# Two products of the first two layers moved from full fp32 to three passes over high and low parts

## What is computed

```python
h = modulate(rms_norm(x, norm1_g[l]), sh1, sc1)
...                                   # projections, gated linear attention -> o_a, differential attention -> o_b2
y_a = o_a @ w_a                       # (512 x 512) @ (512 x 1024)
y_b = o_b2 @ w_b                      # the second branch's product
merged = jax.nn.sigmoid(gate_a) * y_a + jax.nn.sigmoid(gate_b) * y_b
y = merged @ w_o                      # the output product, (512 x 1024) @ (1024 x 1024)
x = x + g1 * y
h = modulate(rms_norm(x, norm2_g[l]), sh2, sc2)
x = x + g2 * hier_moe(h, ...)         # router, then 2 of 32 experts for each token
```

## Time and profile before

| | us |
|---|---|
| median of 3 runs | 3723.69 (3720.17 to 3726.69) |
| the profiled execution's own time | 3723.39 |
| its span in the trace | 3721.7 |
| PE busy | 3159.5 (85%) |
| DVE, ACT, POOL busy | 1131.9, 962.3, 805.8 |
| bytes moved | 663.67 MB |

### The profile page before, as it was taken

How to read it: one execution, slowest core, us unless ns; L and a number is a source line. 1 busy time by engine, 2 the same in 40 slices (tenths; PEclk the granted TensorE clock), 3 DMA queues, 4 the chain that set the end, 5 groups by cost and what they waited for, 6 DMA issues and landing times. The chain is left out here.

```text
span 3721.7 us, 42396 instructions
## 1 busy us (share of the span) xinstructions
PE 3159.5 (85%) x15027; PEld 2046.8 (55%) x15027; DVE 1131.9 (30%) x2001; ACT 962.3 (26%) x1351; POOL 805.8 (22%) x382
## 2 busy tenths in 40 slices
PE   6988987888884798879688777588899998889999
PEld 4764644333332576454433333365688786568877
DVE  4464423111111446431311111134343303434330
ACT  4323311111111522330111111134333323433331
POOL 3311100111111221120011111230243343024432
PEclk7998997899997899889799999789899998989999
DMA  5223332899998122332499999610122331012232
GB/s 209 68 76 126 136 115 91 340 405 409 409 408 311 69 75 99 119 114 92 180 396 408 409 409 407 256 51 31 60 91 80 90 123 51 31 61 91 80 90 69
DMA packets 289710, 663.67 MB, mean 178 GB/s; under 512 B 20190, under 2 KB 114708, under 8 KB 289552
## 3 DMA queue, kind: packets, MB, share of 16 engines
q1 hardware_dynamic: 271680, 623.43, 45.1%
q0 software_dynamic: 17872, 38.14, 2.8%
HBM read 653.64 MB, written 25.69 MB: 183 GB/s over the span
## 5 line engine op out<-in xcount | busy, mean ns | idle before, releaser
L869 PE MATMUL psum<-s_parts 128*128 128x512 f32 (+1 forms) x3744 | 955.2, 407 | 119.5 <-POOL s_parts L757 39.2
L869 PEld LDWEIGHTS psum<-s_parts 128*128 128x128 f32 (+1 forms) x3744 | 723.3, 195 | 327.6 <-issue 85.6
L869 PE MATMUL psum<-s_ring,s_units 128*64 128x512 f32 x3168 | 743.8, 619 | 129.8 <-DMA s_ring<-in_w_expert_in 90.9
L847 POOL TENSOR_TENSOR s_parts<-s_ring,s_parts 128x4096 fp32r<-128x4096 f32 (+2 forms) x52 | 407.8, 7841 | 873.1 <-ACT s_parts L2068 873.1
L869 PEld LDWEIGHTS psum<-s_ring,s_units 128*64 128x64 f32 x3168 | 251.4, 141 | 578.8 <-issue 446.1
L869 PE MATMUL psum<-s_h_low,s_parts 128*128 128x512 f32 (+1 forms) x1872 | 470.7, 392 | 11.2 <-DVE s_hid_low L2039 11.2
L869 PEld LDWEIGHTS psum<-s_h_low,s_parts 128*128 128x128 f32 (+1 forms) x1872 | 350.6, 188 | 96.0 <-DVE s_hid_low L2039 12.1
L869 PE MATMUL psum<-s_units 128*128 (+9 forms) x1520 | 296.5, 412 | 99.1 <-DVE s_gsl L1829 34.3
L757 POOL TENSOR_TENSOR s_parts<-s_ring,s_parts 128x4096 fp32r<-128x4096 f32 (+1 forms) x22 | 180.4, 8200 | 685.0 <-ACT s_parts L2068 685.0
L2068 ACT ACTIVATE s_parts<-s_ring 128x4096 fp32r<-128x4096 f32 (+3 forms) x74 | 237.3, 3209 | 168.4 <-PE psum L869 103.7
L869 PEld LDWEIGHTS psum<-s_units 64*128 64x128 f32 (+3 forms) x1520 | 175.3, 193 | 178.7 <-issue 121.1
(11 more groups left out here) (350 smaller groups left out, 2664.4 us busy)
## 6 DMA issues: line engine op xcount, KB each, us to landing
s_ring<-in_w_expert_in SPq DMA_DIRECT2D x132, 2048.0 KB, 23.5
s_ring<-in_w_expert_out SPq DMA_DIRECT2D x66, 2048.0 KB, 24.6
s_ring<-in_w_in SPq DMA_DIRECT2D x28, 2048.0 KB, 8.8
s_ring<-in_w_ada SPq DMA_DIRECT2D x24, 2048.0 KB, 9.2
s_ring<-in_ffn_w_up SPq DMA_DIRECT2D x40, 1024.0 KB, 6.4
s_ring<-in_ffn_w_down SPq DMA_DIRECT2D x16, 1408.0 KB, 7.0
s_ring<-in_w_out SPq DMA_DIRECT2D x8, 2048.0 KB, 7.8
s_units<-ys_scratch POOLq DMA_DIRECT2D x16, 512.0 KB, 6.4
```

The source lines that it names most:

```text
L847: pool.tensor_tensor(parts[:, s, 0:size], ring[:, s, 0:size], parts[:, 4 + n % 2, 0:size].bitcast(F32), ALU.subtract).then_inc(weights_low ...
L869: return pe.matmul(o, lhsT=lhsT, rhs=rhs, start=start, stop=stop)
```

## The change

`yb` and `wo` become three passes over high and low parts. The activations of `yb` are split by four copies on ACT (into units 8 to 11) and four subtractions on DVE (over `dq` itself); those of `wo` by eight copies on ACT (into `h_hi`) and eight subtractions on DVE (into `h_low`, the memory of `hT`). The three weight blocks `yb`, `wo` 0 and `wo` 1 get their high parts from ACT and low parts from POOL like the others. The squares of the second norm go to units 0 to 7 instead of `hT`. The weights of the first two experts are loaded in another order: the middle blocks of both after `wo` 3, the second expert's other two and one of the first after `wo` 7, and the last one after `rt`.

```diff
-SPLIT_A = [..., ("gb", 0), ("gb", 1)]
+SPLIT_A = [..., ("gb", 0), ("gb", 1), ("yb",), ("wo", 0), ("wo", 1)]
...
+    dq_hi = [hid_low[:, 8 + k, :] for k in range(HEADS)]
+    dq_low = [units_high[:, 2 + k, :] for k in range(HEADS)]
...  SP
-                    sp.wait_ge(TA.done.sem, TA.done_at(l, RA.reader_last(s) if s < 3 else ("gb", 7)))
+                    sp.wait_ge(TA.done.sem, TA.done_at(l, RA.reader_last(s) if s < 3 else last_of_high[s]))
+        last_of_high = {3: ("wo", 7), 4: ("wo", 3), 5: ("wo", 7)}
...
-            for u in (1, 0):
-                expert(l, before * 2, u, u, True)
+            for u, pieces in ((0, (1,)), (1, (1,)), (1, (0, 2)), (0, (2, 0))):
+                expert(l, before * 2, u, u, True, pieces)
...  POOL
-            low_part(10)
+            for n in range(10, len(SPLIT_A)):
+                low_part(n)
...  PE
+            w = [x.rearrange("p k n -> p (k n)").rearrange("p (k n) -> p k n", k=4) for x in block_parts(("yb",))]
+            pe.wait_ge(dq_high.sem, dq_high.at(l, HEADS))
+            pe.wait_ge(dq_lowered.sem, dq_lowered.at(l, HEADS))
             for m in range(8):
-                fm(("yb", m), slot_view(RA.slot(("yb",)), 4, D), P * m, dq, 4)
+                o = opened(("yb", m))
+                for n, (a, rows) in enumerate(((0, dq_hi), (1, dq_hi), (0, dq_low))):
+                    for k in range(HEADS):
+                        last = mm(o, w[a][:, k, tok(m)], rows[k], n == 0 and k == 0, n == 2 and k == HEADS - 1)
+                done(last)
             for m in range(KD):
                 if m % 4 == 0:
+                    w = block_parts(("wo", m // 4))
-                if m == 0:
-                    pe.wait_ge(TA.by(("yb", 7)).sem, TA.freed_at(l, ("yb", 7)))
                 o = opened(("wo", m))
-                for k in range(KD):
-                    last = mm(o, wview(RA, ("wo", m // 4), KD, 512)[:, k, tok(m % 4)], mrg[k], k == 0, k == KD - 1)
+                for n, (a, b) in enumerate(TERMS):
+                    for k in range(KD):
+                        if m == 0 and n == 0:
+                            pe.wait_ge(merged_high.sem, merged_high.at(l, k + 1))
+                        if m == 0 and n == 2:
+                            pe.wait_ge(merged_low.sem, merged_low.at(l, k + 1))
+                        last = mm(o, w[a][:, k, tok(m % 4)], h_parts[b][:, k, :], n == 0 and k == 0, n == 2 and k == KD - 1)
                 done(last)
-            sumsq(("n2",), x_squared, KD)
+            sumsq(("n2",), x_squared, KD, U)
...  DVE
+            for h in range(HEADS):
+                ve.wait_ge(dq_high.sem, dq_high.at(l, h + 1))
+                ve.tensor_tensor(dq_low[h], dq[:, h, :], dq_hi[h].bitcast(F32), ALU.subtract).then_inc(dq_lowered.sem, dq_lowered.more())
+            def low_merged(m):
+                ve.wait_ge(merged_high.sem, merged_high.at(l, m + 1))
+                ve.tensor_tensor(h_low[:, m, :], mrg[m], h_hi[:, m, :].bitcast(F32), ALU.subtract).then_inc(merged_low.sem, merged_low.more())
             for m in range(8):
                 o = done(("yb", m))
...
                 ve.tensor_tensor(mrg[m], mrg[m], T[:, m % 2, :], ALU.add).then_inc(TA.by(("yb", m)).sem, TA.by(("yb", m)).more())
+                if m:
+                    low_merged(m - 1)
+            low_merged(7)
...  ACT
             high_part(10)
+            for h in range(HEADS):
+                ae.wait_ge(head_normed.sem, head_normed.at(l, 13 + h))
+                copy(dq_hi[h], dq[:, h, :]).then_inc(dq_high.sem, dq_high.more())
             for m in range(8):
+                if m == 4:
+                    high_part(11)
                 ae.activation(gate_b[m], done(("gb", m)), ACT.Sigmoid).then_inc(TA.by(("gb", m)).sem, TA.by(("gb", m)).more())
+            high_part(12)
+            for m in range(8):
+                ae.wait_ge(TA.by(("yb", m)).sem, TA.freed_at(l, ("yb", m)))
+                copy(h_hi[:, m, :], mrg[m]).then_inc(merged_high.sem, merged_high.more())
+            high_part(13)
-            squares(KD, lambda k: ae.wait_ge(TA.by(("wo", k)).sem, TA.freed_at(l, ("wo", k))))
+            squares(KD, lambda k: ae.wait_ge(TA.by(("wo", k)).sem, TA.freed_at(l, ("wo", k))), U)
```

More of the change, by code:

```diff
@@ L273, in blocks_b @@
     return [(name, last, s, None) for name, last, s in b]
-SPLIT_A = [("lr",), ("gqk",), ("gv",), ("gg",), ("dq",), ("dk",), ("dv",), ("ga", 0), ("ga", 1), ("gb", 0), ("gb", 1)]
+SPLIT_A = [("lr",), ("gqk",), ("gv",), ("gg",), ("dq",), ("dk",), ("dv",), ("ga", 0), ("ga", 1), ("gb", 0), ("gb", 1), ("yb",), ("wo", 0),
+           ("wo", 1)]
 SPLIT_B = [name for name, *_ in blocks_b()]
@@ L498, in program @@
     weights_made = sig("a_attention_weights", HEADS * NT)
+    dq_high, dq_lowered = sig("a_attention_high", HEADS), sig("a_attention_low", HEADS)
+    merged_high, merged_low = sig("a_merged_high", KD), sig("a_merged_low", KD)
     gates_made = sig("a_branch_a_gates", 3)
@@ L589, in _, with expert @@
         freed_in_m = (m_in_read[0], m_in_read[1], m_down_made)
-        def expert(l, number, e, u, layer_first):
-            for j in range(3):
+        last_of_high = {3: ("wo", 7), 4: ("wo", 3), 5: ("wo", 7)}
+        def expert(l, number, e, u, layer_first, pieces=range(3)):
+            for j in pieces:
                 s = 3 * u + j
                 if layer_first:
-                    sp.wait_ge(TA.done.sem, TA.done_at(l, RA.reader_last(s) if s < 3 else ("gb", 7)))
+                    sp.wait_ge(TA.done.sem, TA.done_at(l, RA.reader_last(s) if s < 3 else last_of_high[s]))
                     settle(sp)
@@ L944, in tm_parts, with sumsq @@
                 done(of_parts(o, lambda a, k: h_parts[a][:, k, tok(t)], lambda b, k: w[b][:, k, :]))
-            def sumsq(name, signal, first):
+            def sumsq(name, signal, first, rows=hT):
                 o = opened(name)
@@ L950, in sumsq @@
                     pe.wait_ge(signal.sem, signal.at(l, first + k + 1))
-                    last = mm(o, ones[:], hT[:, k, :], k == 0, k == KD - 1)
+                    last = mm(o, ones[:], rows[:, k, :], k == 0, k == KD - 1)
                 done(last)
@@ L1134, in _ @@
                 fm_parts(("gb", m), w, P * (m % 4))
-            pe.wait_ge(weights_in_a[RA.slot(("yb",))], RA.landed(l, ("yb",), ("rt",)))
-            pe.wait_ge(head_normed.sem, head_normed.at(l, 16))
+            w = [x.rearrange("p k n -> p (k n)").rearrange("p (k n) -> p k n", k=4) for x in block_parts(("yb",))]
+            pe.wait_ge(dq_high.sem, dq_high.at(l, HEADS))
+            pe.wait_ge(dq_lowered.sem, dq_lowered.at(l, HEADS))
             for m in range(8):
-                fm(("yb", m), slot_view(RA.slot(("yb",)), 4, D), P * m, dq, 4)
+                o = opened(("yb", m))
[3 more added lines that the diff above has]
+                done(last)
             for m in range(KD):
                 if m % 4 == 0:
-                    pe.wait_ge(weights_in_a[RA.slot(("wo", m // 4))], RA.landed(l, ("wo", m // 4), ("rt",)))
-                if m == 0:
-                    pe.wait_ge(TA.by(("yb", 7)).sem, TA.freed_at(l, ("yb", 7)))
+                    w = block_parts(("wo", m // 4))
                 o = opened(("wo", m))
-                for k in range(KD):
-                    last = mm(o, wview(RA, ("wo", m // 4), KD, 512)[:, k, tok(m % 4)], mrg[k], k == 0, k == KD - 1)
+                for n, (a, b) in enumerate(TERMS):
[5 more added lines that the diff above has]
+                        last = mm(o, w[a][:, k, tok(m % 4)], h_parts[b][:, k, :], n == 0 and k == 0, n == 2 and k == KD - 1)
                 done(last)
-            sumsq(("n2",), x_squared, KD)
+            sumsq(("n2",), x_squared, KD, U)
             o = opened(("rt",))
@@ L2084, in done, with squares @@
                 return psum[:, TA.bank(name), :]
-            def squares(first, ready):
+            def squares(first, ready, rows=hT):
                 for k in range(KD):
                     ready(k)
-                    ae.activation(hT[:, k, :], xT[:, k, :], ACT.Square).then_inc(x_squared.sem, x_squared.more())
+                    ae.activation(rows[:, k, :], xT[:, k, :], ACT.Square).then_inc(x_squared.sem, x_squared.more())
             def take_root(name, k, temps=T):
```

## The result

The changed kernel takes **3683.32 us** (median of 4 runs, 3680.11 to 3685.14) against 3721.93 us of the kernel before (median of 4 runs, among them the three given with its profile, 3714.87 to 3726.69): a ratio of 0.9897, 95% interval 0.9879 to 0.9915. The span of its profiled execution is 3682.3 us against 3721.7, 39.4 us less. Faster was forecast, at 3688.4 us with a range of 3678 to 3702.

What follows compares the result with a forecast made beforehand. Weight loading was taken to bound the expert loops, and PE the stretch from `yb` through `wo`. Each layer saves 15.4 - 1.4 + 3.5 = 17.5 us, two 35.0, from 3723.4 to 3688.4 us; range 3678 to 3702.

Steps and rivals of the forecast that it cites:

- Passes: In `yb` and `wo`, outputs take 2.72 and 5.44 us, saving 5.7 and 11.4 us a layer.
- the four-to-three rule: For `yb` and `wo`, three passes cost 0.75 of fp32's four, giving 20.6 us instead of 17.1; not used.
- Splitting ahead of yb, free: Ahead of `yb`, POOL is ready near 491 to 494, DVE near 494, before `yb` can begin at 506.77; costs nothing.
- The stuck additions: During `yb`, DVE's addition of output 1 waits for POOL until 520.4; the stretch ends 15.4 us earlier instead of 18.5.
- The clock: In `wo` 0, PE's idle time ahead lowers its granted clock, costing 1.4 us a layer, between 0 and 2.8.
- `wo` 4's low part, the loads of the first expert: `wo` 4's low part is hidden with 7 us to spare; the last block needs about 8 us after `rt`, PE 31.
- The stores: Behind `rt`, h stores land sooner with fewer loads beside them, so the gather gains 3.5 us a layer, 0 to 4.4.
- The sum: A layer saves 15.4 - 1.4 + 3.5 = 17.5 us, two layers 35.0, giving 3688.4 us.
- The ports don't clash: Rival: in `yb` no addition waits for POOL; 18.5 + 3.5, twice, 3679.4 us; chance 0.12.
- The stores gain nothing and the clock falls further: Rival: no gain behind `rt`, 2.8 us lost in `wo` 0; 15.4 - 2.8, twice, 3698.2 us; chance 0.18.
- No wait took `wo` 4 or the first expert: Rival: late `wo` 1 splits or the first expert's last block swallow the gain, within 0.2%; chance 0.04.
- the clock came back within `wo` 0: Rival: PE stays at the lower clock through `wo`, 23 us lost, twice, 3769 us; chance 0.04.

Runs made afterwards that it cites:

- The kernel with pieces: Changed kernel with POOL's low part of `wo` 0 written as eight subtractions instead of one: median 3678.48 us of 4 runs, ratio 0.9875.
- the added matmuls: Changed kernel plus 18 matmuls filling PE's waits in `wo` 0, output unchanged: 3684.4 us in a single run.
- the kernel before with early loads: Kernel before, with two of the first expert's three blocks loaded after `wo` 3 and `wo` 7: 3711.31 us against 3722.94, ratio 0.9969.
- the kernel with the new order of passes: Changed kernel, POOL's `wo` 0 subtraction in eight, gates 4 to 7 running both high-weight passes first: median 3657.94 us, ratio 0.9827.

## Why the prediction was right, and where it was off

**Passes** (5.7 and 11.4 us a layer): right to the hundredth, 2.72 and 5.44 us an output. The rows of the gates priced them; the four-to-three rule of the Trainium skill ("FP8 and Floating Point Precision", TensorE Precision Notes) would have been 3.5 us a layer too high. The factor is 0.79 here as well.

**Splitting ahead of yb, free:** right. POOL was through at 491.0 (forecast 491 to 494), DVE's four subtractions at 492.7 (forecast 494), and `yb` began at 505.65.

**The stuck additions:** right, mechanism and size. Forecast were one addition of about 7 us ending with POOL, rounds of 2.04 us and the last copy's end 27.0 us after `yb`'s start. It was 7.53 us, 2.02 us and 27.2 us. The kernel with pieces shows that POOL's long instruction was the cause; it saves 17.4 us where 18.5 were reckoned without any wait. DVE still loses 0.3 to 1.1 us in each of seven operations, the last copy ends 24.9 us after `yb`'s start where 24.0 were reckoned, and the 17 matmuls behind it take 0.2 us more than reckoned. With the clock held up (the added matmuls) the stretch saved 15.1 us against the forecast's 15.4.

**The clock** (1.4 us, between 0 and 2.8): the mechanism is shown, and the size was low. It was 1.8 and 2.5 us, nearer to the upper end. Waits of 1.5 us with single matmuls between them did what one gap of 1.76 us hadn't done before.

**`wo` 4's low part, the loads of the first expert:** hidden, as said. High and low part of `wo` 1 were ready at 545.6, `wo` 4 starts at 554.8; the one block issued after `rt` (609.17) landed 7.7 us later.

**The stores** (3.5 us, between 0 and 4.4): this is the term that was mis-sized, 5.6 and 6.0 us. The landing itself came as forecast, 3.9 us for the first store; the whole effect of the loads is 3.5 to 3.8 us in the kernel before with early loads. The failing step is the bound: "the gather waits for its addresses, and these for `routed` (641.57)" held `routed` at its old distance. That distance shrank from 50.22 us behind the sum of squares to 47.85, nearly all of it because PE's counts took 3.85 us in place of 6.0: the granted clock was 1.00 through most of them and not only at their start. The prediction had a row for the stores and none for the counts, and so excluded a gain that was there. Stores now took 3.1 to 3.9 us, of which no row before had one. They lie within 0.7 us of the estimate of 3.2 us from the Trainium skill ("DMA: Bandwidth & Descriptors", Anatomy of one DMA — SWDGE (gpsimd) path).

**The sum:** 35.0 us forecast, 37.8 in the same places: + 4.6 from behind the sum of squares, - 1.8 from the clock in `wo` 0 and small parts of the stretch. Another 1.65 us of the span lie behind the first `gate_up` of layer two, within the scatter of the profiles. So the forecast came out near because errors of both signs stood in it; its largest, the stores, was outside its own bound. That all of it came off the end, as the first paragraph of the prediction argued from the stream of loads, holds for the change; for 3 or 4 us in a single profile it can't be seen.

**The rivals.** "The ports don't clash" is refuted by the 7.53 us. "The stores gain nothing and the clock falls further" was half right on the clock (1.8 and 2.5 us of its 2.8) and wrong on the stores. No wait took `wo` 4 or the first expert, and the clock came back within `wo` 0 in layer one and by its end in layer two.

**Open:** why the clock falls early in the counts in one place and late in another. It was 1.00 when they began in both kernels (630 to 631 before, 616.4 to 618 after the change), although it had stood at 0.50 through the routing product and risen only in the transposes. Before, it was 0.50 from 631.4 on, 0.3 us into the counts; in the changed kernel it fell at 619, 2.5 us into them. In the kernel with the new order of passes both happened, in its two layers.

## What to carry to other kernels

When a product gets cheaper, look at what fed it from beside: a long instruction of one engine can hold up short ones of another that shares nothing with it by data, and cutting it into pieces costs little. Ask of every part of a change whether it needs the others: here the order of three loads was worth 11.6 us (7 to 16) by itself. And order the passes of a split product so that those come first which need only the operand that is ready first.

## What the runs showed of the hardware

Against two POOL subtractions back to back DVE got one turn in between. Of its four subtractions, 0.6 to 0.7 us each when alone, two lasted over 9 us, and the four together took 19.94 us beside POOL's 18.59 us. The first ended 0.55 us after POOL's first instruction (482.14 against 481.59), and the second POOL instruction, begun at 481.55, took 9.44 us where one alone takes 9.03. The timeline in two windows shows the first of each engine and then the rest:

```profile
472.40 9.19 POOL L764 TENSOR_TENSOR s_parts<-s_ring,s_parts 128x4096 fp32r<-128x4096 f32 x1 [32.83 <-ACT s_parts L2095]
472.80 9.34 DVE L1725 TENSOR_TENSOR s_units_high<-s_units,s_hid_low 128x512 fp32r<-128x512 f32 x1
...
481.55 9.44 POOL L764 TENSOR_TENSOR s_parts<-s_ring,s_parts 128x4096 fp32r<-128x4096 f32 x1
482.06 10.68 DVE L1725 TENSOR_TENSOR s_units_high<-s_units,s_hid_low 128x512 fp32r<-128x512 f32 x3
```

With eight short POOL instructions no DVE operation took over 1.78 us. And the granted clock of PE can fall while PE is busy: it went to 0.50 within a stretch of matmuls of 36 columns without a pause. These matmuls took 9.69 us for 64 of them when the clock began at 1.00, and 13.84 us when it was 0.50 throughout.
